# Row factors of an attention spread over partitions by transfers instead of products, and an output bank used in alternating halves

## What is computed

```python
def fox_attention(q, k, v, f_logit):
    logf = jax.nn.log_sigmoid(f_logit.astype(jnp.float32))
    fcum = jnp.cumsum(logf, axis=1)
...
    def one_block(args):
        qi, fqi, bi = args
        scores = jnp.einsum('bqhd,bkhd->bhqk', qi, k,
                            preferred_element_type=jnp.float32) * scale
        bias = jnp.transpose(fqi, (0, 2, 1))[..., None] - fk[:, :, None, :]
        q_pos = bi * Q_BLOCK + jnp.arange(Q_BLOCK)
        mask = key_pos[None, :] <= q_pos[:, None]
        logits = jnp.where(mask[None, None], scores + bias, -jnp.inf)
        p = jax.nn.softmax(logits, axis=-1)
        return jnp.einsum('bhqk,bkhd->bqhd', p, v.astype(jnp.float32))
```

## Time and profile before

| | |
|---|---|
| median of 3 runs | 1962.34 us (1961.93 to 1962.75) |
| the profiled execution | 1960.81 us, span 1959.3 us, clock 0.994 |
| PE busy | 1914.8 us, 98% |
| DVE, ACT, POOL busy | 57%, 36%, 22% |
| attention stage | about 605 to 1580 us |

### The profile page before, as it was taken

How to read it: one execution, slowest core, us unless ns; L and a number is a source line. 1 busy time by engine, 2 the same in 40 slices (tenths; PEclk the granted TensorE clock), 3 DMA queues, 4 the chain that set the end, 5 groups by cost and what they waited for, 6 DMA issues and landing times. The chain is left out here.

```text
span 1959.3 us, 30551 instructions
## 1 busy us (share of the span) xinstructions
PE 1914.8 (98%) x10560; PEld 1625.1 (83%) x10560; DVE 1123.9 (57%) x2142; ACT 707.9 (36%) x1090; POOL 434.9 (22%) x548
## 2 busy tenths in 40 slices
PE   8999999999999999999999999999999989999998
PEld 6878887888887888888888788888888878999997
DVE  4564226654244655646465665565655568777776
ACT  3111013121034555555555655555555532111110
POOL 2927930498000000000000000000000002222322
PEclk9999999999999999999999999999999999999999
DMA  7223225322422141231523515133142276555642
GB/s 191 70 84 116 86 86 199 63 104 107 146 102 93 50 138 55 76 114 47 138 61 87 180 50 139 59 84 108 48 135 65 84 254 215 167 175 170 173 118 87
DMA packets 104569, 221.69 MB, mean 113 GB/s; under 512 B 11001, under 2 KB 56745, under 8 KB 100905
## 3 DMA queue, kind: packets, MB, share of 16 engines
q1 hardware_dynamic: 90736, 161.41, 26.3%
q0 software_dynamic: 12608, 55.19, 10.2%
q10 hardware_dynamic: 1152, 4.19, 0.5%
HBM read 155.09 MB, written 65.08 MB: 112 GB/s over the span
## 5 line engine op out<-in xcount | busy, mean ns | idle before, releaser
L1439 PE MATMUL g_ps<-x_hi,w_lo 128*128 128x512 f32 x768 | 310.1, 404 | 0.0
L1439 PE MATMUL g_ps<-x_hi,w_hi 128*128 128x512 f32 x768 | 309.2, 403 | 0.0
L1355 DVE TENSOR_TENSOR pt_lo<-t_ps,pt_hi 128x512 fp32r<-128x512 f32 (+2 forms) x320 | 190.6, 607 | 140.8 <-ACT pt_hi L1261 140.4
L1439 PE MATMUL g_ps<-x_lo,w_hi 128*128 128x512 f32 x768 | 226.6, 410 | 4.0 <-PEq L1476 2.6
L695 PE MATMUL tile_ps<-x_hi,w_hi 128*128 128x512 f32 x736 | 228.4, 391 | 0.0
L695 PE MATMUL tile_ps<-x_hi,w_lo 128*128 128x512 f32 x736 | 226.7, 389 | 0.0
L695 PE MATMUL tile_ps<-x_lo,w_hi 128*128 128x512 f32 x736 | 226.6, 389 | 0.0
L1261 ACT ACTIVATE pt_hi<-t_ps 128x512 fp32r<-128x512 f32 (+2 forms) x320 | 170.3, 533 | 143.4 <-PE t_ps L1398 138.6
L1293 DVE CUSTOM_DVE_ANT_0 s_sb<-s_ps,f_row 128x512 f32<-128x512 f32 (+2 forms) x320 | 181.8, 604 | 35.0 <-PE s_ps L1387 34.2
L1169 POOL DMA_DIRECT2D mixT<-y_out x63 | 33.8, 536 | 749.5 <-DVE y_out L1307 749.5
L1398 PE MATMUL t_ps<-ident,s_sb 128*128 128x128 f32 x1088 | 172.1, 273 | 9.5 <-DVE pt_lo L1355 5.1
(11 more groups left out here) (288 smaller groups left out, 3569.8 us busy)
## 6 DMA issues: line engine op xcount, KB each, us to landing
w_lo_raw<-in_w_tiles SPq DMA_DIRECT2D x96, 512.0 KB, 3.6
gateT<-g_out SPq DMA_DIRECT2D x96, 256.0 KB, 3.0
gate<-gateT SPq DMA_DIRECT2D x64, 384.0 KB, 4.5
qkvT<-zout SPq DMA_DIRECT2D x24, 512.0 KB, 3.2
x_lo_raw<-in_xT SPq DMA_DIRECT2D x20, 512.0 KB, 8.6
silT<-zout SPq DMA_DIRECT2D x16, 512.0 KB, 2.7
k_ll<-qkvT POOLq DMA_DIRECT2D x16, 512.0 KB, 6.5
q_st<-qkvT POOLq DMA_DIRECT2D x16, 512.0 KB, 8.7
```

The lines of the kernel that those rows point to most:

```text
L1355: dve.tensor_tensor(pt_lo[part], t_ps[n % 2][:, 0:keys].rearrange("p (k q) -> p k q", q=P), pt_hi[part].bitcast(F32), ALU.subtract).then_i ...
L1439: mm = pe.matmul(g_ps[c][:], w[j % 2][:, k, :], x[:, k, c * BANK:(c + 1) * BANK], start=(r == 0), stop=(r == 3 * KT - 1))
```

## The change

1. The two spreading transposes go. GpSimd stores the two columns of `row_inv` of a pair to a new row of DRAM (128 partitions of 8 bytes), in an order that puts the two steps' factors of a partition side by side, and loads that row back onto 64 partitions, into the lower half of the partitions of `y_out`, which grows from 64 to 128 partitions. It does so between the wait for the pair's reciprocals and the store of its output.
2. `o_ps[:, p % 2]` takes the output of pair p. `values` waits for the add of pair p-2, no longer for the multiply of p-1.
3. DVE's add goes to the lower half of a larger `o_low`; the multiply reads it and the loaded factors, both from SBUF, with the factors in steps of two elements. It waits for its own add and for the load. The calls of `output` move from even steps t to odd steps (t = 3 to 15), ahead of the reciprocal.
4. ScalarE's copy stays at even steps and waits also for the add of the pair before.
5. GpSimd no longer waits for each store of `y_out` at once, but ahead of the next load of factors. The next head's `v` is issued right behind `k` and `q`.
6. Two semaphores of the split of `k` and `q` become one.

```diff
@@ spread over GpSimd @@
+            def spread_inverse(h8, p, stored=None):
...
+                pool.wait_ge(inv_ready, h8 + (p + 1))
+                pool.sem_inc(passed)
+                row = scr["inv"][bass.ds(h8 + p, 1)]
+                pool.dma_start(row.rearrange("o (q a) -> q (o a)", a=2), row_inv[:, 2 * p:2 * p + 2]).then_inc(inv_stored, 16)
+                if stored is not None:
+                    pool.wait_ge(y_stored, stored)
+                    pool.sem_inc(passed)
+                pool.wait_ge(inv_stored, h8 * 16 + 16 * (p + 1))
+                pool.sem_inc(passed)
+                pool.dma_start(y_out[p % 2][HD:P], row.partition_broadcast(HD)).then_inc(inv_loaded, 16)
...
             with pool.Fori(0, HEADS - 1) as h:
-                for p in range(6):
-                    store_y(h * 8, h * HD + 2 * P, p)
+                spread_inverse(h * 8, 0)
+                for p in range(1, 7):
+                    spread_inverse(h * 8, p, store_y(h * 8, h * HD + 2 * P, p - 1))
                 pool.wait_ge(s_full, h * S_PIECES + S_PIECES)
                 load_kq(h * HD + HD)
-                store_y(h * 8, h * HD + 2 * P, 6)
                 load_v(h * HD + HD)
+                spread_inverse(h * 8, 7, store_y(h * 8, h * HD + 2 * P, 6))
                 pool.wait_ge(s_free, h * S_PIECES + S_PIECES)
                 load_f(h + 1)
-                store_y(h * 8, h * HD + 2 * P, 7)
+                pool.wait_ge(y_stored, store_y(h * 8, h * HD + 2 * P, 7))
+                pool.sem_inc(passed)
@@ ScalarE @@
                 act.wait_ge(o_full, at(8, p + 1))
-                act.activation(o_low[:], o_ps[HD:P, 0, :], ACT.Copy).then_inc(o_low_ready, 1)
+                act.wait_ge(o_sum, at(8, p + 2))
+                act.sem_inc(passed)
+                act.activation(o_low[0:HD], o_ps[HD:P, p % 2, :], ACT.Copy).then_inc(o_low_ready, 1)
@@ DVE @@
                 dve.wait_ge(o_low_ready, at(8, p + 1))
-                dve.wait_ge(y_free, at(8, p + 1))
+                if p:
+                    dve.wait_ge(y_ready, at(8, p))
+                dve.sem_inc(passed)
+                dve.tensor_tensor(o_low[HD:P], o_ps[0:HD, p % 2, :], o_low[0:HD], ALU.add).then_inc(o_sum, 1)
+                dve.wait_ge(o_sum, at(8, p + 3))
+                dve.wait_ge(inv_loaded, at(128, 16 * (p + 1)))
+                dve.sem_inc(passed)
                 y = y_out[p % 2]
-                dve.tensor_tensor(y[:], o_ps[0:HD, 0, :], o_low[:], ALU.add).then_inc(o_sum, 1)
-                dve.wait_ge(o_sum, at(8, p + 1))
-                dve.tensor_tensor(y[:], y[:], o_ps[0:HD, 1, :], ALU.mult).then_inc(y_ready, 1)
+                dve.tensor_tensor(y[0:HD].rearrange("d (a q) -> d a q", a=2),
+                                  o_low[HD:P].rearrange("d (a q) -> d a q", a=2),
+                                  y[HD:P].rearrange("d (q a) -> d a q", a=2), ALU.mult).then_inc(y_ready, 1)
...
-                    if t % 2 == 0 and t >= 2:
+                    if t % 2 == 1 and t >= 3:
                         output(at, t // 2 - 1)
@@ PE @@
                 pe.wait_ge(t_lo, at(PT_USES, pieces_to(2 * p + 1) + 2))
-                if p:
-                    pe.wait_ge(y_ready, at(8, p))
+                pe.wait_ge(o_sum, at(8, p + 1))
...
-                        pe.matmul(o_ps[:, 0, q], v_st[:, k, :], pt[:, k, q], start=(k == 0 and j == 0),
-                                  stop=(k == last_key and j == 1))
-                pe.wait_ge(inv_ready, at(8, p + 1))
-                pe.sem_inc(passed)
-                for a in range(2):
-                    last = pe.transpose(o_ps[0:HD, 1, a * P:(a + 1) * P],
-                                        row_inv[:, 2 * p + a:2 * p + a + 1].broadcast_to([P, HD]), ident[:])
+                        last = pe.matmul(o_ps[:, p % 2, q], v_st[:, k, :], pt[:, k, q], start=(k == 0 and j == 0),
+                                         stop=(k == last_key and j == 1))
                 last.then_inc(o_full, 1)
```

More of the change, by code:

```diff
@@ L99, in __init__ @@
         self.g_out = [at(f"g_out{i}", 5, [P, BANK], skip=4 * i * BANK) for i in range(NCH)]
-        self.y_out = [at(f"y_out{i}", 5, [HD, 2 * P], skip=4 * (2 * BANK + i * 2 * P)) for i in range(2)]
+        self.y_out = [at(f"y_out{i}", 5, [P, 2 * P], skip=4 * (2 * BANK + i * 2 * P)) for i in range(2)]
         self.ln_g = at("ln_g", 5, [P, D])
@@ L1067, in stage_attend @@
         (x2_hi, x2_split, gb_loaded, gb_half, gw_split_hi, gw_split, g_done, g_ready, k_hi,
-         k_lo, q_hi_tmp, q_hi, q_lo, s_full, s_free, max_ready, p_ready, t_full, t_hi, t_lo, inv_ready, o_full,
-         o_low_ready, o_sum, y_ready) = (
+         kq_low, q_hi_tmp, q_hi, s_full, s_free, max_ready, p_ready, t_full, t_hi, t_lo, inv_ready, o_full,
+         o_low_ready, o_sum, y_ready, inv_stored, inv_loaded) = (
             sem(n) for n in (
-                "x2_hi", "x2_split", "gb_loaded", "gb_half", "gw_split_hi", "gw_split", "g_done", "g_ready", "k_hi", "k_lo", "q_hi_tmp", "q_hi", "q_lo", "s_full", "s_free", "max_ready",
-                "p_ready", "t_full", "t_hi", "t_lo", "inv_ready", "o_full", "o_low_ready", "o_sum", "y_ready"))
+                "x2_hi", "x2_split", "gb_loaded", "gb_half", "gw_split_hi", "gw_split", "g_done", "g_ready", "k_hi", "kq_low", "q_hi_tmp", "q_hi", "s_full", "s_free", "max_ready",
+                "p_ready", "t_full", "t_hi", "t_lo", "inv_ready", "o_full", "o_low_ready", "o_sum", "y_ready", "inv_stored",
+                "inv_loaded"))
         kq_loaded, v_loaded, f_loaded = kept.kq_loaded, kept.v_loaded, kept.row_loaded
@@ L1150, in _ @@
             row = (HEADS - 1) * HD + 2 * P
-            sp.dma_start(scr["mixT"][row:row + HD, 14 * P:], y_out[1][:]).then_inc(last_y_stored, 16)
+            sp.dma_start(scr["mixT"][row:row + HD, 14 * P:], y_out[1][0:HD]).then_inc(last_y_stored, 16)
         @block.gpsimd
@@ L1164, in load_f @@
                 pool.dma_start(f_row[:], scr["fcum"][bass.ds(h, 1)].partition_broadcast(P)).then_inc(f_loaded, 16)
+            def spread_inverse(h8, p, stored=None):
[9 more added lines that the diff above has]
+                pool.dma_start(y_out[p % 2][HD:P], row.partition_broadcast(HD)).then_inc(inv_loaded, 16)
             def store_y(h8, row, p):
                 pool.wait_ge(y_ready, h8 + (p + 1))
+                pool.sem_inc(passed)
                 pool.dma_start(scr["mixT"][bass.ds(row, HD), p * 2 * P:(p + 1) * 2 * P],
[L1170 to L1174, removed]
+                               y_out[p % 2][0:HD]).then_inc(y_stored, 16)
+                return h8 * 16 + 16 * (p + 1)
             for u in range(2):
@@ L1177, in _ @@
             with pool.Fori(0, HEADS - 1) as h:
-                for p in range(6):
-                    store_y(h * 8, h * HD + 2 * P, p)
+                spread_inverse(h * 8, 0)
+                for p in range(1, 7):
+                    spread_inverse(h * 8, p, store_y(h * 8, h * HD + 2 * P, p - 1))
                 pool.wait_ge(s_full, h * S_PIECES + S_PIECES)
                 load_kq(h * HD + HD)
-                store_y(h * 8, h * HD + 2 * P, 6)
                 load_v(h * HD + HD)
+                spread_inverse(h * 8, 7, store_y(h * 8, h * HD + 2 * P, 6))
                 pool.wait_ge(s_free, h * S_PIECES + S_PIECES)
                 load_f(h + 1)
-                store_y(h * 8, h * HD + 2 * P, 7)
-            for p in range(7):
-                store_y((HEADS - 1) * 8, (HEADS - 1) * HD + 2 * P, p)
+                pool.wait_ge(y_stored, store_y(h * 8, h * HD + 2 * P, 7))
+                pool.sem_inc(passed)
+            spread_inverse((HEADS - 1) * 8, 0)
+            for p in range(1, 8):
+                spread_inverse((HEADS - 1) * 8, p, store_y((HEADS - 1) * 8, (HEADS - 1) * HD + 2 * P, p - 1))
         def phases(eng, before, body):
```

17 lines of the change are left out of this document (10 added, 7 removed).

## The result

| | before | after |
|---|---|---|
| median on one chip | 1961.93 us (1959.12 to 1962.75, 5 runs) | 1971.22 us (1969.15 to 1976.66, 5 runs) |
| ratio | | 1.0053, 95% interval 1.0041 to 1.0064 |
| the profiled execution | 1960.81 us, span 1959.3 | 1975.32 us, span 1973.8 |

The change makes the kernel slower by 0.5%, where 1957.0 us, range 1948 to 1963, was forecast. The profiled execution of after lies 4 us above the median, so what follows adds up to 14.5 us of span, of which the medians show about 9.

A forecast was written before the change was run, and what follows sets the result against it. The attention stage was taken to be bound by instruction slots on PE (TensorE). Removing spreading products (-13.9 us) and longer waits for DVE (+8.6) summed to -5.3 us, from the median 1962.34 to 1957.0 us, range 1948 to 1963.

The forecast's parts named there:

- What is removed from PE: Spreading products after each pair of query-tile steps: removal gives back 0.22 us a pair, 64 pairs, 13.9 us taken.
- lower bound: PE saving of 12.8 us in all, if the transition to the next transpose costs 0.02 us more than taken.
- What moves on DVE: Add and multiply moved to odd steps, ahead of `pt_lo`: 0.83 us inserted, 8 x (0.83 + 0.25) = 8.6 us given back.
- both places: Of a head's query-tile steps 0 to 15, PE waits longer for `pt_lo` at 13 (0.83 us) and 11 (0.25 us).
- all is given back: Rival, 7%: add and multiply with two waits take DVE 1.3 us instead of 0.83; net +2, 1964 us.
- What is added on GpSimd and the queues: 64 stores of 1 KB and 64 loads of 64 KB on GpSimd's queue: in time for their readers, costing nothing.
- round trip: Reciprocals stored to DRAM and loaded back on GpSimd's queue: each transfer taken to land 2.0 us after issue.
- late round trip: Rival, 10%: factors late at step 5, once the store lands later than 5.7 us after issue; at 8.5 us, 1979.
- slack: At step 5, DVE's idle 1.68 us and 2.1 us more cover a factors' load landing up to 3.7 us late.
- even steps: DVE no longer sits between `pt_hi` and `pt_lo` there; PE waited for DVE at none, so nothing is won.
- would show it wrong: Signs: `y_out` waiting at step 5 or 3, add-to-multiply well above 0.5 us, no growth at 13, waits at even steps or between heads.

The follow-up runs named there:

- e6: Kernel before without the two spreading products and without a replacement (multiply reads `o_low`, rows not normalised): 1953.93 us, ratio 0.9950.
- e3: Kernel before with only DVE's add and multiply moved from even to odd steps: 1970.10 us, ratio 1.0032.
- e5: Changed kernel with the wait for the loaded factors ahead of the add instead of between add and multiply: 1974.30 us, ratio 1.0055.
- e11: Kernel of e5 with add and multiply kept on partitions 0 to 63, rows not normalised: 1968.96 us, ratio 1.0032.
- e1: Changed kernel with the load of the next head's `v` moved back behind the transfers of pairs 6 and 7: 1969.42 us, ratio 1.0029.
- e7: Changed kernel with `v` late as in e1 and, at odd steps 9 to 15, add and multiply ahead of the next step's logits: 1954.42 us, ratio 0.9952.
- e9: Changed kernel with one edit: at steps 9, 11, 13 and 15 add and multiply ahead of the next step's logits; `v` stays early: 1958.52 us, ratio 0.9969.

## Why the prediction was wrong

- **"What is removed from PE"** was right: 0.22 us a pair forecast; 0.22 in the row of step 12, 0.20 as a mean in e6, near the lower bound that the prediction gave (12.8 us). The records' length of 0.272 was no guide. The whole saving is 12.5 us instead of 13.9.
- **"What moves on DVE"** had both places right and mis-sized the insertion: 0.83 us forecast, 1.22 measured. The parts at step 13: 0.77 for the add and the multiply in that place (e3; 0.79 by the earlier trace rows); 0.25 because they go over to partitions 64 to 127 and back, so that the split ends before the add starts and the multiply before the reciprocal (e5 to e11: 1.02 to 0.77); 0.20 for the wait for the own add on a row of its own, with the factors' wait behind it (after to e5). The forecast had the first, cost operands in SBUF "the same" without looking at which partitions, and bounded the last by 0.09, from waits for another engine that were already on instructions. So 0.83 + 0.25 = 1.08 us a head became 1.22 + 0.51 = 1.73, and 13.1 instead of 8.6 in the run. Against the saving of 12.5 that alone turns the forecast gain of 5.3 into a loss of 0.6. It is the rival "all is given back", priced at 1.3 us and given 7%; it was held cheap because today's add is handed over in 0.03 us, which it is on one set of partitions with nothing between.
- **"What is added on GpSimd and the queues"** was wrong in what it left out. It asked whether each transfer would be in time for its own reader, and for `v` found that it "no longer waits". It didn't ask whose transfer shares the path in those microseconds: SP's weights, a queue that the change doesn't name, and behind them on ScalarE the split of `k` and `q`. The Trainium skill (DMA: Bandwidth & Descriptors, the section on issuing engines not being separate DMA queues) says that transfers of all issuing engines run on the same DMA engines and interleave; the trace agrees, 9.2 us for a load that took 4, and this sentence of the page bore on the case more than the one on small pieces that the prediction quoted. That is 5 us in the medians (after to e1, net of e1's new wait for `v`), and 10.2 at the starts of heads 4 to 7 in the profiled execution.
- The **round trip** was mis-sized too and cost little. Landing of the reciprocals' store (line 1173), 64 in after:

```profile
DMA to landing us min/median/max: 3.0/3.5/9.4
```

3.5 us instead of 2.0, and the factors' load 2.6 instead of 2.0. That is below the 5.7 us of the store from which the late round trip would decide: the multiply at step 5 waits 1.6 to 2.6 us in every head, within the slack that the prediction had worked out, and PE loses nothing there. 18 multiplies waited, 23.8 us in sum, nearly all behind slack.
- The **even steps** were costed at nothing gained, and e3's head beside its step 13 agrees: moving the output off them gives nothing back.
- What "would show it wrong" named waits between heads and an add-to-multiply step above 0.5 us. Both came.

## What to carry to other kernels

An operation that is moved costs most just ahead of the one that a saturated engine waits for; the same two operations a few rows earlier on DVE were free (e7), and that decided the sign of the whole change (after against e9, which differ in nothing else). When a load is issued earlier, look for what else lands in that window on any queue, and what an in-order engine does behind it. And cost an operation on DVE by a row of the same form: the same partitions as its neighbours, and the same waits.

## What the runs showed that was not expected

- On DVE, add and multiply of 64 x 256 cost 0.77 us where they start on the partitions of their neighbours (e11) and 1.02 where they don't (e5), with equal durations in the records (0.41 and 0.42).
- A 1 KB store of 128 pieces of 8 bytes is slower than a 64 KB one: 3.5 us in the median to land, against 2.3 for the store of `y_out` in the same run (2.0 before), and 9.4 behind a burst.
- Three transfers of two queues, of 1, 64 and 512 KB, issued within 1 us, all take 7.8 to 9.4 us, with the loads of `k`, `q` and `v` (five of 512 KB) issued 7 to 10 us ahead of them.
- A PE wait of 2.08 us was followed by a window at a granted clock of 0.83, and the gate products behind it took 3.27 us for eight instead of 2.15: the wait was paid about one and a half times. Behind a wait of 1.22 us at head 6 the clock stayed at 1.00 and nothing was added.
- A gain or loss in the attention stage isn't the whole difference: the merge stage of the profiled execution is 1.0 us shorter than before in after and 2.9 longer in e6. Projections, untouched in all kernels, differ by up to 5.4 us from before between profiled executions (e7's), so a difference of a few us must be read stage by stage, and its size taken from the medians.
